# A gated linear attention stage: norm bands of a head from last to first, squares ahead of the gate logs, and low parts in four GpSimd operations

## The reference

```python
logits = einsum(glr, gla_w_gate) + gla_b_gate
log_a = log_sigmoid(logits) / 16            # one per token, direction, key channel
o_f, sg_f = gla_scan(qh, kh, vh, log_a[:, :, 0], gla0[:, 0])
o_b, sg_b = gla_scan(flip(qh), flip(kh), flip(vh), flip(log_a[:, :, 1]), gla0[:, 1])
o = o_f + flip(o_b)
mu = mean(o); var = mean(square(o - mu))    # over the 256 values of a head
on = (o - mu) * rsqrt(var + 1e-5)
y_gla = on * gla_norm_g * silu(r)           # r: another projection of the input
```

## Time and profile before

| | |
|---|---|
| median of 3 runs | 2983.23 us |
| profiled execution | 2990.47 us, of it span 2988.7 us |
| PE busy | 2812.8 us, 94% of the span |
| DVE, ACT, POOL busy | 1819.2 (61%), 1137.7 (38%), 812.1 (27%) us |
| mean granted TensorE clock | 0.976 |

### The profile page before, as it was taken

The page is one execution under the profiler, slowest core; times in us unless marked ns, Lnnn a source line. Parts: engine busy times, 40 slices in busy tenths (PEclk is TensorE's granted clock), DMA queues, the critical chain, the costliest instruction groups (busy, mean ns, idle before and its releaser), DMA issues. The chain is left out here.

```text
span 2988.7 us, 41328 instructions
## 1 busy us (share of the span) xinstructions
PE 2812.8 (94%) x16768; PEld 2747.4 (92%) x16768; DVE 1819.2 (61%) x2422; ACT 1137.7 (38%) x1709; POOL 812.1 (27%) x381
## 2 busy tenths in 40 slices
PE   6999997899999798999979999999999999999996
PEld 6999997789889798999979999999999999999996
DVE  7688885455444699999956546788642232223226
ACT  2798984343434323444433101003652112211224
POOL 0223321101110135555504344343111111111123
PEclk9999998999999899999989999999999999999998
DMA  5112111001110344444435446444111111111111
GB/s 225 54 52 67 62 48 60 29 24 50 49 33 25 100 154 164 121 121 121 121 111 178 169 142 206 143 133 165 36 36 43 43 43 43 43 43 43 43 42 65
DMA packets 111177, 257.78 MB, mean 86 GB/s; under 512 B 20960, under 2 KB 54752, under 8 KB 110752
## 3 DMA queue, kind: packets, MB, share of 16 engines
q1 hardware_dynamic: 100608, 214.19, 23.0%
q10 hardware_dynamic: 10400, 41.24, 3.8%
HBM read 199.01 MB, written 56.37 MB: 85 GB/s over the span
## 5 line engine op out<-in xcount | busy, mean ns | idle before, releaser
L2621 PE MATMUL bank<-yhi,w_hi 128*128 128x384 f32 x1560 | 525.6, 337 | 5.8 <-POOL w_lo L2551 3.5
L2621 PE MATMUL bank<-ylo,w_hi 128*128 128x384 f32 x1560 | 522.1, 335 | 0.0
L2621 PE MATMUL bank<-yhi,w_lo 128*128 128x384 f32 x1560 | 522.0, 335 | 0.0
L2551 POOL TENSOR_TENSOR w_lo<-w_raw,w_hi 128x1024 fp32r<-128x1024 f32 x69 | 169.3, 2454 | 681.7 <-ACT w_hi L2729 681.7
L182 POOL TENSOR_TENSOR w_lo<-w_raw,w_hi 128x1024 fp32r<-128x1024 f32 x57 | 170.4, 2990 | 605.7 <-ACT w_hi L177 605.5
L2588 PE MATMUL bank<-yhi,w_hi 128*128 128x384 f32 x864 | 291.1, 337 | 28.4 <-POOL w_lo L169 24.0
L2621 PEld LDWEIGHTS bank<-yhi,w_hi 128*128 128x128 f32 x1560 | 293.7, 188 | 9.9 <-POOL w_lo L2551 4.4
L2621 PEld LDWEIGHTS bank<-ylo,w_hi 128*128 128x128 f32 x1560 | 293.5, 188 | 1.2 <-issue 0.3
L2621 PEld LDWEIGHTS bank<-yhi,w_lo 128*128 128x128 f32 x1560 | 293.5, 188 | 0.0
L2588 PE MATMUL bank<-ylo,w_hi 128*128 128x384 f32 x864 | 289.8, 335 | 0.0
L2588 PE MATMUL bank<-yhi,w_lo 128*128 128x384 f32 x864 | 289.8, 335 | 0.0
(11 more groups left out here) (433 smaller groups left out, 6618.8 us busy)
## 6 DMA issues: line engine op xcount, KB each, us to landing
w_raw<-in_mlp_units SPq DMA_DIRECT2D x64, 512.0 KB, 3.6
w_raw<-in_s_units SPq DMA_DIRECT2D x32, 512.0 KB, 4.5
mrg_scr<-in_w_ada_rows SPq DMA_DIRECT2D x32, 512.0 KB, 3.7
mid_gates<-gate ACTq DMA_DIRECT2D x24, 576.0 KB, 3.3
gt<-mid_gates SPq DMA_DIRECT2D x24, 576.0 KB, 4.1
w_raw<-in_gla_units SPq DMA_DIRECT2D x25, 512.0 KB, 3.9
w_raw<-in_lru_units SPq DMA_DIRECT2D x24, 512.0 KB, 4.0
x<-in_x_t SPq DMA_DIRECT2D x16, 576.0 KB, 10.0
```

The source lines that it names most:

```text
L2551: pool.tensor_tensor(WLO[SLOT[u]], S.raw[u % 2], WHI[SLOT[u]].bitcast(F32), ALU.subtract).then_inc(S.split_done, 1)
L2621: mm = pe.matmul(out, wt[SLOT[u]][:, w], r[:, k, band_cols(b)], start=(k == first and y == 0), stop=(k == last and y == 2))
```

## The change

Three things. First, all heads normalise their bands in the order 2, 1, 0 (before, only the last head did, and heads 0 to 2 went 0, 1, 2); the bands of `r` are projected in that order too. So `square` need not wait for the whole head, only for the last step that touches its band. Second, for heads 0 to 2 `square` moves one step up, to steps 0, 1, 2 of the next head, and inside step 1 ahead of `log_gates`; DVE's `spread` moves one step up as well, and `spread`, `normalise` and `resonate` now stand ahead of `forget`, `accumulate`, `keys`, `ended` and `queries` within a step. Third, POOL's subtraction of a unit is four instructions of 256 columns in place of one of 1024; only the last raises `split_done`. This is so for the 24 units that POOL splits inside this stage.

```diff
--- before.py
+++ after.py
@@ -773,7 +773,7 @@
         LAST = HEADS - 1
         FREED_AT = {n: s for s, (d, n) in enumerate(STEPS) if d}
         VALUES = [list(range(NPAIR))] + [[0, 8, 7, 6, 5, 4, 1, 2, 3]] * LAST
-        SILU = [(w, b) for w in range(2) for b in range(NB)]
+        SILU = [(w, b) for w in range(2) for b in (2, 1, 0)]
         SILU_LAST = [(w, b) for b in (2, 1, 0) for w in range(2)]
         BEFORE = -1
 
@@ -788,12 +788,13 @@
                 SLOT += [0, 2, 1, 0]
         UNITS += [("r", LAST, 0), ("r", LAST, 1)]
         SLOT += [0, 2] + [1, 0]
-        BANDS = [(u, b) for u, (kind, h, w) in enumerate(UNITS) if kind != "v" for b in range(NB)]
-        FIRST_BAND = {UNITS[u]: n for n, (u, b) in enumerate(BANDS) if b == 0}
+        BANDS = [(u, b) for u, (kind, h, w) in enumerate(UNITS) if kind != "v"
+                 for b in ((2, 1, 0) if kind == "r" else range(NB))]
+        FIRST_BAND = {UNITS[u]: n for n, (u, b) in enumerate(BANDS) if n % NB == 0}
         PRE_BANDS = 3 * NB
 
-        def norm_band(h, i):
-            return i if h < LAST else NB - 1 - i
+        def norm_band(i):
+            return NB - 1 - i
 
         def step_band(h, s):
 
@@ -970,14 +971,17 @@
                         pool.memset(probs[d][s][:], 0.0).then_inc(const_done, 1)
                 for u in range(AHEAD + 1, len(SLOT)):
                     pool.wait_ge(S.hi_done, u + 1)
-                    pool.tensor_tensor(wlo[SLOT[u]][:], S.raw[u % 2], whi[SLOT[u]][:].bitcast(F32),
-                                       ALU.subtract).then_inc(S.split_done, 1)
+                    for x in range(0, UW, UW // 4):
+                        part = slice(x, x + UW // 4)
+                        ins = pool.tensor_tensor(wlo[SLOT[u]][:, part], S.raw[u % 2][:, part], whi[SLOT[u]][:, part].bitcast(F32),
+                                                 ALU.subtract)
+                    ins.then_inc(S.split_done, 1)
 
             @block.tensor
             def _(pe):
                 def band(n):
                     u, b = BANDS[n]
-                    if b == 0:
+                    if n % NB == 0:
                         pe.wait_ge(S.split_done, u + 3)
                     pe.wait_ge(band_free, n - 1 if n >= AHEAD * NB + 2 else n - AHEAD * NB + 1)
                     out = band_bank(n)
@@ -1108,7 +1112,7 @@
                         act.wait_ge(o_mm, NSTEP * LAST + NPAIR)
                         ins = act.activation((qd[0], ki[0])[w][:, cols], src, ACT.Silu)
                     else:
-                        m = 2 * NB * h + NB * w + b
+                        m = 2 * NB * h + NB * w + n % NB
                         if m >= 2:
                             act.wait_ge(rm_done, m - 1)
                         ins = act.activation(rr[m % 2][:], src, ACT.Silu)
@@ -1156,11 +1160,8 @@
 
                 def square(h, b):
 
-                    y = norm_band(h, b)
-                    if h < LAST:
-                        act.wait_ge(o_done, NSTEP * (h + 1))
-                    else:
-                        act.wait_ge(o_done, NSTEP * h + FREED_AT[max(NB * y, 1)] + 1)
+                    y = norm_band(b)
+                    act.wait_ge(o_done, NSTEP * h + FREED_AT[max(NB * y, 1)] + 1)
                     if NB * h + b >= 2:
                         hb, bb = divmod(NB * h + b - 2, NB)
                         act.wait_ge(item_mm, ITEM["var", hb, 0, bb] + 1)
@@ -1193,12 +1194,12 @@
                             evac_item(key)
                         for u in units_after(NSTEP * h + s):
                             unit_hi(u)
+                        if h and s < NB:
+                            square(h - 1, s)
                         if s == 1:
                             log_gates(h, 1)
                         if s == 4:
                             decays(h, 1)
-                        if h and 1 <= s < 1 + NB:
-                            square(h - 1, s - 1)
                         if h < LAST:
                             if s == 10:
                                 log_gates(h + 1, 0)
@@ -1336,7 +1337,7 @@
                     w, b = (SILU if h < LAST else SILU_LAST)[j]
                     cols = slice(b * BW, (b + 1) * BW)
                     gain = (qd[0], ki[0])[w][:, cols] if h == LAST else rr[(2 * NB * h + j) % 2][:]
-                    dve.wait_ge(band_free, FIRST_BAND["r", h, w] + b + 1)
+                    dve.wait_ge(band_free, FIRST_BAND["r", h, w] + NB - b)
                     ov = o[h % 2][:, w, cols]
                     dve.tensor_tensor(ov, ov, gain, ALU.mult).then_inc(rm_done, 1)
 
@@ -1365,8 +1366,12 @@
                         for kind, hh, d, x in step_items(h, s):
                             if kind == "value":
                                 value(hh, x)
-                        if h and 2 <= s < 2 + NB:
-                            spread(h - 1, s - 2)
+                        if h and 1 <= s < 1 + NB:
+                            spread(h - 1, s - 1)
+                        if h and 3 <= s < 3 + NB:
+                            normalise(h - 1, s - 3)
+                        if h and 4 <= s < 4 + 2 * NB:
+                            resonate(h - 1, s - 4)
                         if s == 3:
                             forget(h, 1)
                         if s == 4:
@@ -1379,10 +1384,6 @@
                             queries(h, 1)
                         if s == 8:
                             ended(h, 1, 2)
-                        if h and 3 <= s < 3 + NB:
-                            normalise(h - 1, s - 3)
-                        if h and 4 <= s < 4 + 2 * NB:
-                            resonate(h - 1, s - 4)
                         if h < LAST:
                             if s == 12:
                                 forget(h + 1, 0)
```

## The result

The changed kernel takes 2954.34 us (median of 4 runs, 2950.49 to 2957.39) against 2983.06 (4 runs, 2980.91 to 2985.93): ratio 0.9900, 95% interval 0.9884 to 0.9916. It is 28.7 us faster; 2955.0 was predicted, in a range of 2948 to 2966.

The account below looks back on a forecast made before the run. PE, busy 94% of the span, was taken to bound the kernel; 24.6 us at three boundaries, 2.9 in head 0 and 0.7 before it sum to 28.2 us, giving 2955.0 us from the median 2983.23, range 2948 to 2966.

Parts of the forecast that it names:

- Boundaries: At three head boundaries, PE's steps 1 to 7 were to take 38 us instead of 46, saving 24.6 us in all.
- variance wait: In step 2 after a head boundary, PE's first "var" item waits 2.76 us; it was to wait for nothing.
- step 6 wait: At a head boundary, PE's `outputs` of step 6 waits 2.93 us for `advance`; this wait was to go.
- New wait in step 5: At each boundary, PE was to wait 1.1 us for `advance`, which follows `accumulate` on DVE, in place of none.
- Half clock: At each boundary, stretches at granted clock 0.50 were to go with the two waits, giving 3.6 of the 8.2 us.
- Pieces: POOL's subtraction pieces of 256 columns were taken at 0.6 us each, with 1.24 us as upper bound.
- Head 0: PE's 7.74 us wait behind DVE's copy and subtraction was to fall to about 4.9, saving 2.8 to 2.9 us.
- pieces that don't let DVE in: Rival: POOL keeps the port, `resonate` ends 1.5 us later at each boundary; saving 23 us, in the forecast's lower half.
- pieces as dear as whole operations: Rival, chance 0.05: 256 columns cost nearly as much as 1024, four times 2.4 us a unit; slower, 2993 us.
- a gain that comes back: Rival, chance 0.05: something after the boundary or at the next stage's start holds PE; saving under 6 us, about 2981.
- the larger saving: Rival, chance 0.12: no step 5 wait, head 0's blocking wholly gone, its half clock shorter; saving 35 us, time 2948.
- rival 1: Chance 0.18: PE waits more in step 5, 2.5 us a boundary plus about 1.5 for the clock; saving 16, time 2967.

Follow-up runs that it names:

- two half experiments: Order-only kernel with normalise and resonate back behind the gate work: 2968.8 us; order-only kernel with square and spread back one step: 2967.4 us.
- squares up only: The order-only kernel with normalise and resonate put back behind forget, accumulate, keys, ended and queries: 2968.8 us, ratio 0.9947.
- order only: The changed kernel with POOL's subtraction of a unit as one instruction of 1024 columns again: 2956.8 us, ratio 0.9909.

## Why the prediction was right

- **Boundaries.** Predicted 8.2 us each, 24.6 in all; measured 8.0, 8.3 and 8.0, 24.2. The new order came out as laid over the old times. With both traces aligned at `outputs` of step 1 (4.14 us apart), the first `resonate` ends at 661.3 as I had it, `advance` of step 5 starts at 664.7 where I had 664.8, and `outputs` of step 6 at 671.4 where I had 671.3. The last step, 6 to 7, took 6.04 us where I took 5.9. The order alone gives 23.2 of it; I had put the share of the pieces there at 1.5 us, and it is 1.0. The two half experiments show that both halves are needed, and that the variance wait and the step 6 wait have separate causes.
- **New wait in step 5.** Predicted 1.1 us, measured 1.08, three times; that `accumulate` makes it is shown by moving it.
- **Half clock.** That the stretches behind the two waits go with them held at all three boundaries. I took the third to be like the others; before, it had a second "var" wait in place of one stretch, of nearly the same price. That the clock falls behind such a wait each time does not hold: in squares up only it did not fall behind 3.51 us.
- **Pieces.** I took 0.6 us, a quarter of the whole operation, and the median is 0.74. That left out a cost per instruction: four minimum times are 2.86 us against some 2.38 for one, about 0.16 us for each further instruction.
- **Head 0.** Predicted 2.8 to 2.9 us off the wait, measured 3.2. DVE was blocked for 0.34 and 0.47 us (alone the copy takes 0.17 and the subtraction 0.76), less each time than the whole piece that I had put there. Before head 0 PE's two waits together fell by 0.4 us, from 4.3 to 3.9; 0.7 were predicted.
- **Missed.** At step 13 of heads 0 to 2 POOL's unit, now 0.4 us longer, reaches into the scan, and PE waits 1.28 us instead of 0.86: 1.3 us in all. I had put POOL's longer time at nothing. With one instruction a unit (order only) the wait is 0.86, with the pieces alone 1.28.
- **Rivals.** A wait above 3 us in step 5, pieces that don't let DVE in, pieces as dear as whole operations, and a gain that comes back were all seen not to be so. Of the larger saving, only the shorter half clock in head 0 showed itself, and in other runs: in the changed kernel it still lasted 9 us behind the wait. The range was said to hold nearly all of rival 1, whose own time, 2967, lies outside it.

The sum of 28.2 us stands against 26.4 in the stage, which the parts measured make up: 24.2 + 3.2 + 0.4 - 1.3 = 26.5. The whole moved by 28.7 us with an interval of about 4.8 to either side, so the last two us of agreement are luck.

## What to carry to other kernels

When a chain goes over three engines, place each link by laying the new order over the times of the old trace: the length of the chain's group on the slowest link (here 5.60 us of table loads and activations on ACT) and the one long instruction that stands ahead of it say where the next wait will be. Then move that instruction to where its engine waits anyway; here that was worth another 10 us. A long wait of PE (here 2.8 us and more) should be priced with what its clock may do afterwards. Between versions that differ by 1 or 2 us the stretch between two fixed rows is a better measure than the whole time, with the clock beside it.

## What the runs showed of the hardware

- A GpSimd subtraction of 128, 256, 512 and 1024 columns has medians of 0.46, 0.74, 1.30 and about 2.4 us. Cut into pieces that stand ready one behind the other, it lets a waiting DVE operation in between them: the same `resonate` of 384 columns, 0.56 us by itself, took 2.54, 1.42, 0.87 and 0.59 us beside one, two, four and eight.
- TensorE's granted clock stood at 0.50 for 3 to 14 us at single waits of 2.76 to 7.74 us in the heads, and behind pairs close together before head 0 (3.06 and 1.23, 1.96 and 1.93, 1.42 and 1.80 us). It did not fall behind single waits of 1.0 to 1.4 there. Behind one wait of 3.51 us and three of 2.8 it did not fall either, while in the same runs it fell behind others of 3.5 and of 2.8. At the start of the next stage PE waits for ACT's gate: the clock fell in the eight profiles where this wait was 2.4 to 3.2 us, and not in the five where it was 1.1 to 2.0. What decides between these was not tried.
